# A mixture of experts' weight panels asked for in order of use from the first unit, in place of the order in which ring places come free

## What is computed

```
logits = h @ router_w + router_b             # 256 tokens, 32 experts
top_logit, top_idx = top_k(logits, 4)        # each token goes to 4 experts
gate = softmax(top_logit)
for each expert e, over the tokens that chose it:
    hid = x @ w1[e] + b1[e]                  # 1024 -> 2048
    glu, lin = clipped halves of hid
    act = glu * sigmoid(1.702 * glu) * (lin + 1)
    out += gate * (act @ w2[e] + b2[e])      # 1024 -> 1024
```

## Time and profile before

| | |
|---|---|
| Median of 3 runs | 2422.96 us (2420.51 to 2423.84) |
| The profiled execution | 2425.65 us |
| its span in the trace | 2423.8 us |
| TensorE busy | 2284.3 us (94% of the span) |
| Expert weights | 192 transfers of 2048 KB, of 619.02 MB in all |
| Matmuls of the experts (L2775, L2805) | 3072 |

### The profile page before, as it was taken

The page is one execution under the profiler, slowest core; times in us unless marked ns, Lnnn a source line. Parts: engine busy times, 40 slices in busy tenths (PEclk is TensorE's granted clock), DMA queues, the critical chain, the costliest instruction groups (busy, mean ns, idle before and its releaser), DMA issues. The chain is left out here.

```text
span 2423.8 us, 30917 instructions
## 1 busy us (share of the span) xinstructions
PE 2284.3 (94%) x12895; PEld 1512.8 (62%) x12895; DVE 682.1 (28%) x1476; ACT 398.6 (16%) x832; POOL 73.2 (3%) x81
## 2 busy tenths in 40 slices
PE   8999999999899999998799999999999999979998
PEld 7888788877688877887633333333333333358886
DVE  4242200134400032626322222222322222252232
ACT  1210110014200012224211111111111111123331
POOL 0110100000000000011000000000000000000000
PEclk9999999999999999999899999999999999999999
DMA  6334644455844454310679999999999999943422
GB/s 266 123 122 141 227 155 148 149 208 185 318 175 155 143 196 147 131 37 2 279 326 428 428 428 428 428 428 428 426 428 428 428 428 428 428 168 101 164 70 87
DMA packets 60986, 619.02 MB, mean 255 GB/s; under 512 B 6784, under 2 KB 8064, under 8 KB 12288
## 3 DMA queue, kind: packets, MB, share of 16 engines
q1 hardware_dynamic: 59184, 611.08, 63.1%
q10 hardware_dynamic: 1712, 6.63, 0.8%
HBM read 616.63 MB, written 1.05 MB: 255 GB/s over the span
## 5 line engine op out<-in xcount | busy, mean ns | idle before, releaser
L391 PE MATMUL ps<-x_res,ring 128*128 128x256 f32 x2560 | 568.3, 384 | 21.8 <-ACT x_res L962 12.8
L391 PEld LDWEIGHTS ps<-x_res,ring 128*128 128x128 f32 x2560 | 490.3, 193 | 92.7 <-issue 17.4
L2775 PE MATMUL ps<-expert_ring,moe_xg 128*64 128x512 f32 x1024 | 229.0, 595 | 26.2 <-DMA expert_ring<-we_dram 26.1
L391 PE MATMUL ps<-first_arena,ring 128*128 128x256 f32 x1088 | 236.5, 379 | 1.4 <-DMA ring<-w_o_dram 1.4
L2775 PE MATMUL ps<-ring,moe_xg 128*64 128x512 f32 x1024 | 230.1, 599 | 5.6 <-DMA ring<-we_dram 5.6
L2805 PE MATMUL ps<-expert_ring,mix_y 128*64 128x512 f32 x1024 | 226.8, 596 | 0.0
L391 PEld LDWEIGHTS ps<-first_arena,ring 128*128 128x128 f32 x1088 | 206.8, 190 | 29.6 <-DMA ring<-w_o_dram 1.9
L391 PE MATMUL ps<-third_h,ring 128*128 128x256 f32 x768 | 175.4, 385 | 5.2 <-ACT third_h L274 3.9
L2775 PEld LDWEIGHTS ps<-expert_ring,moe_xg 128*64 128x64 f32 x1024 | 71.2, 137 | 173.2 <-issue 124.2
L2775 PEld LDWEIGHTS ps<-ring,moe_xg 128*64 128x64 f32 x1024 | 72.3, 138 | 153.6 <-issue 126.9
L391 PEld LDWEIGHTS ps<-third_h,ring 128*128 128x128 f32 x768 | 147.1, 193 | 27.7 <-issue 6.5
(11 more groups left out here) (545 smaller groups left out, 1911.0 us busy)
## 6 DMA issues: line engine op xcount, KB each, us to landing
expert_ring<-we_dram SPq DMA_DIRECT2D x128, 2048.0 KB, 22.0
ring<-we_dram SPq DMA_DIRECT2D x64, 2048.0 KB, 24.5
ring<-w_in_dram SPq DMA_DIRECT2D x55, 1024.0 KB, 4.9
ring<-ffn_up_dram SPq DMA_DIRECT2D x44, 1024.0 KB, 4.8
ring<-ada_dram SPq DMA_DIRECT2D x36, 1024.0 KB, 4.9
ring<-w_out_dram SPq DMA_DIRECT2D x16, 1024.0 KB, 5.1
ring<-ffn_dn_dram SPq DMA_DIRECT2D x16, 1024.0 KB, 4.9
ring<-ple_g_dram SPq DMA_DIRECT2D x8, 1024.0 KB, 5.8
```

Source lines behind the costliest of these rows:

```text
L391: mm = pe.matmul(core.ps[:, t % BANKS, 0:TOK], w[:, k * PANEL + c * P:k * PANEL + c * P + P], sources[panel](k0 + k), start=(k0 + k == 0), ...
L2775: mm = pe.matmul(ps[out, bank, :], xg[:, j % 4, j // 4, :], w[:, bank * D + at:bank * D + at + 512], start=False, stop=(j == 7))
```

## The change

The loop of turns 1 to 8 with the order in which places come free goes away, and `in_turn`, the order of use, runs from turn 1. Nothing else of the kernel changes: the same 192 transfers, the same places, the same waits of TensorE.

```
-                with sp.Fori(1, AHEAD) as v:
-                    load(v * 2, v * 2 - 2, twice, 0, v * 2)
-                    load(v * 2 - 1, v * 2 - 2, once, 1, v * 2 - 1)
-                    load(v * 2 + 1, v * 2 - 1, twice, 1, v * 2 + 1)
-                    load(v * 2, v * 2 - 1, once, 0, v * 2)
-
                 def in_turn(v, before, even, odd):
                     load(v * 2 - 1, v * 2 - 2, once, 1, before)
                     load(v * 2, v * 2 - 2, twice, 0, even)
                     load(v * 2, v * 2 - 1, once, 0, even)
                     load(v * 2 + 1, v * 2 - 1, twice, 1, odd)
-                with sp.Fori(AHEAD, E // 2 - 1) as v:
+                with sp.Fori(1, E // 2 - 1) as v:
                     in_turn(v, v * 2 - 1, v * 2, v * 2 + 1)
...
-PANELS, PAIRS, TWICE, AHEAD = 12, 6, 2, 9
+PANELS, PAIRS, TWICE = 12, 6, 2
```

## The result

The changed kernel takes 2431.78 us (median of 7 runs, 2430.88 to 2441.0) against 2424.86 us for the kernel before in its own 7 runs beside it. The ratio is 1.0036, with a 95% interval of 1.0023 to 1.0050: slower by 8.7 us, between 5.6 and 12.1. The ratio is worked out over all the runs of both kernels and not from the two medians, which are 6.9 us apart. The forecast was +9.0, or 2432.0 us.

What follows compares the result with a forecast made beforehand. Transfers at 428 GB/s were taken as the bound, TensorE some 7% behind. Two pairs moved later cost +9.8, less 0.8 for an earlier q4: 2422.96 + 9.0 = 2432.0 us, range 2429.0 to 2437.0.

Steps and rivals of the forecast that it cites:

- main term: Start of the experts' stage: two pairs not moved by 1244 must be moved later by a never idle queue, +9.8 us.
- the five quick units: Units 17 to 21, without a wait for q3, become units of 29.42 us instead of 27.45; the same +9.8 us.
- The start: First transfer of the loop waits for unit 1's q2 place: issued at 1230.9 rather than 1224.0, 6.9 us later.
- The term of -0.8: At q4 of unit 1, the briefly empty queue lets it land up to 1.6 us earlier; middle taken, -0.8 us.
- waits for q3: TensorE waits 1.2 us in every unit from 6 to 31, 26 in place of 21.
- The absolute times: Unit 16 begins at 1679.3 or up to 1.6 earlier, unit 22 at 1854.9, the last scatter at 2149.6.
- the order does nothing: Rival: the start is absorbed by slack in the transfers or q0 isn't asked for that early; 2423.0 us, chance 0.04.
- The faster case: Rival: early q0 and q1 cause the waits of units 6 to 16, which would go; -11.9, 2411.1 us, chance 0.03.
- A queue that runs dry again: Rival: the queue empties in each of units 1 to 5, 15.5 us on top; 2447.5 us, chance 0.03.
- each dry moment: Whenever the transfer queue runs dry, it costs 8.0 - 4.9 = 3.1 us.
- The range: Whole kernel: 8.2 to 12.9 us slower, with some 2 us for the medians, 2429.0 to 2437.0 us.

Runs made afterwards that it cites:

- experiment 4: Kernel before, order kept, with a wait of SP for unit 0's q2 ahead of the loop, so the first transfer goes out later; ratio to before 1.0022, +5.3 us.
- experiment 1: Kernel before with the order of places held for turn 1 alone, the order of use from then on; ratio to before 1.0015, +3.6 us.
- 3: Changed kernel with q0 and q1 of unit 2 asked for first, everything behind them in the order of use; ratio to before 1.0026, +6.3 us.
- 5: Kernel before with the order of places held for turns 1 to 14, the order of use only for the last; ratio to before 1.0018, +4.4 us.

## Why the prediction was right

**The bound and the main term.** Transfers at 428 GB/s set the pace, two pairs were not moved at the start, and nothing takes them back: 2 x 4.90 = 9.8 forecast, 9.7 measured in the stage without lag. It shows in both places that the prediction named, the missing 2 x 2 MB ahead of q4 of unit 1 and the five quick units that are gone. The cost has two parts that the runs tell apart: the late start by itself is 6.6 (experiment 4), and the rest is the hole ahead of q4 of unit 1, which the late-started kernel doesn't have: 2 x (428 - 29) / 428 + 2 x (428 - 156) / 428 = 3.1 us from 1238 to 1242. The runs add what the prediction hadn't said: the two are the same loan only as long as it is kept until TensorE's own lead is spent (experiments 1 and 3) and called back before the end (5).

**The start.** The first transfer went out 12.1 us behind TensorE's first matmul (1214.44 to 1226.52) for 5.8 before, 6.3 later and not 6.9. The 0.6 is TensorE's: the same 48 matmuls took 11.85 us for 12.48 with a granted clock of 0.66 over their first 4 us for 0.50, that is with more of them at the upper level of 2.4 GHz.

**The term of -0.8.** Its size was about right, its cause wasn't. The prediction had the hole give q4 a faster landing, up to 1.6 us, and it was 2.0: 7.6 for 9.6. But without the lag the hole gave back nothing that repeats, 9.7 for 9.8. What made q4 slow before was the last engine: in the five traces of the two kernels q4 lands 9.6, 8.3, 9.1, 7.6 and 7.7 us after its issue, and the median engine reports after 7.2 to 7.3 in all of them. The stages with lag, 891.8 before on the mean of three and 900.5 after on two, are 8.8 apart, next to the measured ratio's 8.7; so the term is the difference between lags, 2.8 before and 1.8 after, and it varies between executions. That the sum came within 0.3 us of the measured 8.7 is in part luck: -0.8 was the middle of a range for another cause. So is the median, 2431.78 for 2432.0: the three runs from which the forecast started have a median of 2422.96, the seven beside the changed kernel 2424.86.

**Waits and times.** 25 waits for q3 were there, for 26 forecast; TensorE stayed ahead one unit longer, to unit 6. The spacing of units 17 to 20 is as forecast. The absolute times came 5.8 to 6.6 us early: unit 16 at 1672.70 for 1679.3, unit 22 at 1849.12 for 1854.9, the last scatter at 2143.77 for 2149.6. Of this, 4.4 us is that this execution began unit 1 at 1243.27 and not at 1247.65, which no row of before could tell. At unit 16 the other 2.2 is the lag there, 1.7 us for 3.9.

**The rivals.** That the order does nothing is out by the interval. The faster case is out: the waits of units 7 to 16 are as long as before, 1.2 us for q3, and the whole is slower. A queue that runs dry again didn't come in the changed kernel, at 428 GB/s from 1260 on, but it is no fancy: experiments 1 and 3 made it happen, two holes each. Its price was wrong, though. The prediction took 3.1 us for each dry moment, the difference between two times to landing; in experiment 1 a hole costs the time for which the queue stands idle, 2.4 and 3.5 us.

**The range.** Its upper end is 0.9 us short of its own terms: 2422.96 + 12.9 + 2 is 2437.9, not 2437.0. The measured 2431.78 lies inside by both.

## What to carry to other kernels

Where transfers are the bound, ask what the queue does while the consumer is still ahead: each us for which it has a free place and asks for nothing is lost for good, and a place that comes free early is worth filling early even with data needed late. Only until the lead is spent, though: the order of use has to come back some units ahead of the end, or the bound moves to the consumer. Measure such an effect between two events inside the stage, with the last engine's lag taken off, since whole executions of one kernel here differed by up to 11 us.

## What the hardware showed that was not expected

The last of the 16 DMA engines can report 1.4 to 3.6 us behind the median one until the end of a saturated stream, within 0.3 us of the same lag over some 170 transfers. In the first trace of the kernel before it is one engine alone, with the next at 0.6; in the third four others are 1.1 to 1.9 behind. A hole of 2 to 4 us in the stream brings the lag back to 0.3 to 0.7. And a transfer of 2 MB cut into two of 1 MB costs 0.08 to 0.09 us more of a saturated queue.
